# MLP down projections of an encoder trunk as 2x2 blocks with seven products (Strassen), MLP in four quarters of ff, weight sums on GpSimd

## The reference, cut to what matters

```python
D_MODEL, SEQ, DEPTH, D_FF = 1024, 512, 2, 4096      # float32 throughout

def squared_relu_mlp(h, w_in, w_out):
    u = jnp.square(jax.nn.relu(jnp.einsum('bsd,df->bsf', h, w_in)))
    return jnp.einsum('bsf,fd->bsd', u, w_out)

def reference(x, ...):
    for i in range(DEPTH):
        h = rms_norm(x, mix_norm[i])
        x = x + (neighbourhood_attention if i % 2 == 0 else sliding_window_gqa)(h, ...)
        h = rms_norm(x, mlp_norm[i])
        x = x + squared_relu_mlp(h, mlp_w_in[i], mlp_w_out[i])
    return rms_norm(x, final_norm)
```

## Time and profile before

| what | value |
|---|---|
| time, median of 3 runs | 1123.13 us (1123.12 to 1123.52) |
| profiled execution, first to last instruction (span) | 1121.9 us |
| time of runs less span | 1.2 us |
| PE busy | 1111.0 us, 5412 matmuls |
| DVE, ACT, POOL busy | 624.5, 521.0, 144.0 us |
| granted TensorE clock, mean | 0.998 |

### The profile page before, as it was taken

How to read it: one execution, slowest core, us unless ns; L and a number is a source line. 1 busy time by engine, 2 the same in 40 slices (tenths; PEclk the granted TensorE clock), 3 DMA queues, 4 the chain that set the end, 5 groups by cost and what they waited for, 6 DMA issues and landing times.

```text
span 1121.9 us, 16256 instructions
## 1 busy us (share of the span) xinstructions
PE 1111.0 (99%) x5412; PEld 925.6 (83%) x5412; DVE 624.5 (56%) x997; ACT 521.0 (46%) x921; POOL 144.0 (13%) x252
## 2 busy tenths in 40 slices
PE   8999999999999999999999999999999999999997
PEld 6888888888888888888888888888888888888886
DVE  7778887764442234443436799875443223444333
ACT  6777767654431124442325788744442112443222
POOL 6544332240000000000000244200000000000000
PEclk9999999999999999999999999999999999999999
DMA  6332322342223322222232223232222232222222
GB/s 225 101 93 75 112 75 74 94 121 94 93 94 100 104 96 94 93 93 96 91 112 91 65 86 85 72 122 94 93 93 94 96 102 102 93 93 94 93 93 94
DMA packets 37122, 109.09 MB, mean 97 GB/s; under 512 B 6544, under 2 KB 10928, under 8 KB 37088
## 3 DMA queue, kind: packets, MB, share of 16 engines
q1 hardware_dynamic: 32176, 100.74, 26.7%
q0 software_dynamic: 4768, 7.90, 3.1%
q10 hardware_dynamic: 144, 0.02, 0.0%
HBM read 105.93 MB, written 2.70 MB: 97 GB/s over the span
## 4 chain that ended last, share of the span: by engine, by line
PE 97%; DVE 1%; issue 0%; DMA 0%; ACT 0%; SPq 0%; DVEq 0%; ACTq 0%
PE acc L490 27%; PE acc L492 27%; PE acc L491 27%; PE acc L524 3%; PE om_ps L808 2%; PE pt_ps L795 1%; PE om_ps L643 1%; PE s_ps L606 1%; PE pt_ps L627 1%; PE s_ps L784 1%; PE om_ps L596 1%; PE s_ps L785 1%; PE s_ps L490 1%; PE s_ps L492 1%; PE s_ps L491 1%
## 5 line engine op out<-in xcount | busy, mean ns | idle before, releaser
L909 ACT CAST w_hi<-w_raw 128x1024 fp32r<-128x1024 f32 x179 | 188.0, 1050 | 388.1 <-PE acc L492 382.4
L1238 DVE TENSOR_TENSOR w_lo<-w_raw,w_hi 128x1024 fp32r<-128x1024 f32 x177 | 216.3, 1222 | 143.6 <-ACT w_hi L909 143.6
L490 PE MATMUL acc<-h_hi,w_hi 128*128 128x512 f32 x736 | 291.3, 396 | 0.9 <-DVE w_lo L1238 0.9
L492 PE MATMUL acc<-h_hi,w_lo 128*128 128x512 f32 x736 | 286.9, 390 | 0.0
L491 PE MATMUL acc<-h_lo,w_hi 128*128 128x512 f32 x736 | 286.5, 389 | 0.0
L490 PE MATMUL acc<-u_hi,w_hi 128*128 128x512 f32 (+1 forms) x624 | 240.4, 385 | 0.0
L492 PE MATMUL acc<-u_hi,w_lo 128*128 128x512 f32 (+1 forms) x624 | 239.5, 384 | 0.0
L491 PE MATMUL acc<-u_lo,w_hi 128*128 128x512 f32 (+1 forms) x624 | 239.4, 384 | 0.0
L490 PEld LDWEIGHTS acc<-h_hi,w_hi 128*128 128x128 f32 x736 | 138.3, 188 | 31.6 <-DVE w_lo L1238 1.6
L492 PEld LDWEIGHTS acc<-h_hi,w_lo 128*128 128x128 f32 x736 | 138.1, 188 | 29.2
L491 PEld LDWEIGHTS acc<-h_lo,w_hi 128*128 128x128 f32 x736 | 138.5, 188 | 28.3 <-issue 0.7
(11 more groups left out here) (171 smaller groups left out, 1119.8 us busy)
## 6 DMA issues: line engine op xcount, KB each, us to landing
w_raw<-in_wstream SPq DMA_DIRECT2D x180, 512.0 KB, 3.3
bias_pairs<-rpb_reversed POOLq DMA_DIRECT2D x64, 62.0 KB, 2.4
bias_pairs<-t_shifted POOLq DMA_DIRECT2D x64, 48.0 KB, 2.1
x_res<-in_xT SPq DMA_DIRECT2D x8, 256.0 KB, 5.9
vT<-inverse_sums SPq DMA_DIRECT2D x16, 128.0 KB, 3.0
out_y<-x_res SPq DMA_DIRECT2D x10, 128.0 KB, 1.8
out_y<-x_res SPq DMA_DIRECT2D x3, 256.0 KB, 2.4
inverse_sums<-sw_turned SPq DMA_DIRECT2D x32, 1.0 KB
```

The source lines that it names most:

```text
L490: nc.tensor.matmul(dst, a[0], b[0], start=start, stop=False)
L492: return nc.tensor.matmul(dst, a[1], b[0], start=False, stop=stop)
L909: nc.scalar.copy(w_hi[:, c.odd, :], w_raw[:, c.odd, :]).then_inc(w_hi_made, 1)
L1238: nc.vector.tensor_tensor(w_lo[:, c.odd, :], w_raw[:, c.odd, :], f32(w_hi[:, c.odd, :]), ALU.subtract).then_inc(w_split, 1)
```

## The change

The two halves of ff become four quarters of 8 hidden tiles. In each quarter the down projection (8 output tiles, 8 hidden tiles, 512 tokens) is a 2x2 block product: a group is two output tiles (i = 0, 1), the hidden tiles are four pairs, and the tokens are two halves of 256 (j = 0, 1). Instead of eight block products a group makes seven runs, with sums of weight blocks and of hidden blocks as operands. A run is 4 pairs x 3 matmuls, 256 tokens wide. Four groups make a quarter, 28 runs, in the order written by `run_order`. Some runs resume the bank of an earlier one, so that their sum is what DVE reads.

- POOL (`first_sums`) makes four sums of 128x512 for each group from the two raw chunks. ACT (`group_high`) casts 3.5 chunks' worth for a group instead of 2, in four pieces; DVE (`group_low`) subtracts as much.
- For each pair of hidden tiles DVE makes the sums (`hidden_sums`, three instructions) and low parts in three pieces (`hidden_low`), ACT the high parts in three pieces (`hidden_high`).
- DVE takes seven results of 128x256 for each group (`take_run`). Run 1's results gather in a buffer of their own; POOL adds them to x in the last quarter (`add_first_run`).
- Hidden stages have 9, 8, 8 and 7 tiles: each but the last ends with the first tile of the next quarter. Its result is taken in the last cycle of the runs.
- Raw weights of groups 0 and 2 go to a new buffer `d_raw`, those of groups 1 and 3 to `w_raw`. The high and low weights have two halves, which chunks and groups use in turn.
- After the first MLP two chunks of the sliding-window projections run interleaved (`two_after_norm`), and POOL adds the squares for that norm (`add_square`). The loads of the sliding-window biases for the first two pairs move on POOL's queue from before the first MLP to behind it.
- The end: run 3 of the last group has a bank of its own and comes last; the final norm's statistics of tiles 6 and 7 come from it and the runs before.
- All MLP loops are unrolled. Several buffers of the attention stages share room with the new ones.

```diff
+IN_STAGES = [range(0, 9), range(9, 17), range(17, 25), range(25, 32)]
+WEIGHTS_PIECE = {1: 1, 2: 1, 5: 2, 6: 2, 7: 3, 3: 3, 4: 4}
+HIDDEN_PIECE = {1: 1, 2: 2, 3: 2, 4: 3, 5: 3, 6: 3, 7: 3}
+def run_order(m, q):
+    order = [(0, 1), (0, 6), (0, 5), (0, 2), (0, 7)]
+    for g in range(1, GROUPS):
+        order += [(g, 1), (g, 6), (g - 1, 4), (g - 1, 3), (g, 5), (g, 7), (g, 2)]
+    order += [(3, 3), (3, 4)]
+    if (m, q) == (1, 3):
+        order[-9:] = [(3, 1), (3, 6), (2, 4), (3, 2), (3, 7), (2, 3), (3, 4), (3, 5), (3, 3)]
+    return order
...
+            def load_group(m, q, g):
+                gi = 16 * m + 4 * q + g
+                if gi >= 2:
+                    sp.wait_ge(d_split, 4 * gi - 4)
...
+                if g == 1:
+                    sp.wait_ge(w_split, (CH_MLP0, CH_MLP1)[m] + IN_STAGES[q][-1] + 1)
+                for i in range(2):
+                    sp.dma_start(raw_rows(q, g)[:, i, :], wstream[out_place(m, q, 2 * g + i)]).then_inc(d_landed[g % 2][i], 16)
...
+            def first_sums(m, q, g):
+                gi, raw = 16 * m + 4 * q + g, raw_rows(q, g)
+                if gi >= 1:
+                    pool.wait_ge(d_split, 4 * gi - 1)
+                pool.wait_ge(d_landed[g % 2][1], 16 * (gi // 2 + 1))
+                nc.gpsimd.tensor_tensor(w_sums[:, 0:QUAD], raw[:, 1, 0:QUAD], raw[:, 1, QUAD:2 * QUAD], ALU.add).then_inc(sums_made, 1)
...
+                nc.gpsimd.tensor_tensor(w_sums[:, QUAD:2 * QUAD], w_sums[:, 0:QUAD], raw[:, 0, 0:QUAD], ALU.subtract).then_inc(sums_ended, 1)
+                nc.gpsimd.tensor_tensor(w_sums[:, 2 * QUAD:3 * QUAD], raw[:, 0, 0:QUAD], raw[:, 1, 0:QUAD],
+                                        ALU.subtract).then_inc(sums_made, 1)
+                pool.wait_ge(sums_ended, 2 * gi + 1)
+                nc.gpsimd.tensor_tensor(w_sums[:, 3 * QUAD:4 * QUAD], raw[:, 0, QUAD:2 * QUAD], w_sums[:, QUAD:2 * QUAD],
+                                        ALU.subtract).then_inc(sums_ended, 1)
...
+            def mlp(m):
...
+                for q in range(QUARTERS):
+                    ends = q == QUARTERS - 1
+                    first_sums(m, q, 0)
+                    first_sums(m, q, 1)
+                    for g in range(GROUPS):
+                        if ends:
+                            add_first_run(m, g)
+                            if g and m == 0:
+                                add_square(2, 2 * g - 2)
+                                add_square(2, 2 * g - 1)
+                        if g < GROUPS - 2:
+                            first_sums(m, q, g + 2)
...
+            def run(m, q, g, r):
...
+                pe.wait_ge(d_split, 4 * gi + WEIGHTS_PIECE[r])
+                before = {2: 1, 7: 6, 4: 7, 3: 5}
...
+                elif r in before:
+                    pe.wait_ge(run_taken, RUN[quarter, g, before[r]])
+                elif gi >= 2:
+                    pe.wait_ge(run_taken, RUN[(gi - 2) // 4, (gi - 2) % 4, {1: 2, 6: 4, 5: 3}[r]])
+                for k in range(PAIRS_K):
+                    if g == 0:
+                        pe.wait_ge(u_split, 3 * (4 * quarter + k) + HIDDEN_PIECE[r])
...
+                    ins = product(bank, (parts[:, 0, :], parts[:, 1, :]), (uh[:, k, other, :], ul[:, k, other, :]),
+                                  k == 0 and (parted or r not in before), k == PAIRS_K - 1, r in before and not parted)
...
+            def hidden_sums(m, n):
...
+                nc.vector.tensor_tensor(t_sums[:, 0:4:2, :], hidden[:, at:at + 2, FEW:SEQ], first.rearrange("p (j t) -> p j t", j=2),
+                                        ALU.subtract).then_inc(hidden_summed, 1)
...
+                nc.vector.tensor_tensor(t_sums[:, 1, :], second[:, FEW:SEQ], t_sums[:, 0, :], ALU.subtract).then_inc(hidden_summed, 1)
...
+                nc.vector.tensor_tensor(t_sums[:, 3, :], second[:, 0:FEW], t_sums[:, 1, :], ALU.subtract).then_inc(hidden_summed, 1)
...
+            def hidden_low(m, n):
...
+                nc.vector.tensor_tensor(ul[:, k, 0, :], first[:, 0:FEW], f32(uh[:, k, 0, :]), ALU.subtract).then_inc(u_split, 1)
...
+                nc.vector.tensor_tensor(ul[:, k, 1:3, :], second.rearrange("p (j t) -> p j t", j=2), f32(uh[:, k, 1:3, :]),
+                                        ALU.subtract).then_inc(u_split, 1)
...
+                nc.vector.tensor_tensor(ul[:, k, 3:7, :], t_sums, f32(uh[:, k, 3:7, :]), ALU.subtract).then_inc(u_split, 1)
...
+                    for i, (g, r) in enumerate(run_order(m, q)):
...
+                        slot = i - at
+                        if cycle < GROUPS - 1:
+                            if slot in (1, 2) or slot == 3 and cycle == 0:
+                                group_low(m, q, cycle + 1, slot)
+                            elif cycle and slot in (4, 5):
+                                group_low(m, q, cycle + 1, slot - 1)
...
+                        take_run(m, q, g, r)
+            def two_after_norm(c, g, n):
...
+                for k in range(6):
+                    part(c + 1, g + 1, h_tile, [k])
+                    if k == 2:
+                        statistics(n)
+                for k in range(6, KT):
+                    pe.wait_ge(h_low, KT * n + k + 1)
+                    part(c, g, h_tile, [k])
+                    part(c + 1, g + 1, h_tile, [k])
```

More of the change, by code:

```diff
@@ L697, in output_projection @@
                     part(At(ch + EARLY + n), At(gr + EARLY + n), u_tile, ALL)
[L699 to L725, removed]
@@ L727, in last_statistics, with first_statistic_of_last @@
-            def last_statistics(n):
[L729 to L732, removed]
+            def first_statistic_of_last():
+                pe.wait_ge(h_split, KT * NORMS - 2)
+                pe.wait_ge(pool_filled, 4)
+                for n in range(2):
+                    for b in range(2):
+                        nc.tensor.matmul(last_stats[n], sqsum[:, (2 * n + b) * P:(2 * n + b + 1) * P],
+                                         pick[:, 1 - b:3 - b], start=b == 0, stop=False)
@@ L733, in last_statistics @@
+            def last_statistics(n):
+                pe.wait_ge(x_prepared, KT * NORMS + 2 * n)
+                for k in range(2):
+                    for b in range(2):
+                        ins = nc.tensor.matmul(last_stats[n], last_square[:, k, (2 * n + b) * P:(2 * n + b + 1) * P],
+                                               pick[:, 1 - b:3 - b], start=False, stop=k == 1 and b == 1)
                 ins.then_inc(stat_done, 1)
@@ new lines, in mlp @@
+            def mlp(m, norm):
+                c0 = (CH_MLP0, CH_MLP1)[m]
+                for q, stage in enumerate(IN_STAGES):
+                    for n in stage:
+                        c = At(c0 + n)
+                        if n == 0:
+                            part_after_norm(c, c, norm)
+                        else:
+                            part(c, c, h_tile, ALL, weights=(chunk_parts(0, q % 2)[:, c.odd, :], chunk_parts(1, q % 2)[:, c.odd, :]))
+                    for g, r in run_order(m, q):
+                        if (m, q, g, r) == (1, 3, 3, 3):
+                            first_statistic_of_last()
+                            last_statistics(0)
+                        run(m, q, g, r)
+                if m == 1:
+                    spread_rstd(0)
+                    last_statistics(1)
+                    spread_rstd(1)
@@ new lines, in square, with hidden_high @@
+            def square(m, n):
+                c = (CH_MLP0, CH_MLP1)[m] + n
+                at = hidden[:, n % 4, :]
+                act.wait_ge(acc_taken, c + 1)
+                nc.scalar.activation(at, at, ACT.Square).then_inc(squared, 1)
+            def hidden_high(m, n):
+                pair, k = 16 * m + n // 2, n // 2 % PAIRS_K
+                first, second = hidden[:, n % 4 - 1, :], hidden[:, n % 4, :]
+                act.wait_ge(squared, 32 * m + n + 1)
+                if n >= 8:
+                    act.wait_ge(run_done, RUNS * (4 * m + n // 8))
+                nc.scalar.copy(uh[:, k, 0, :], first[:, 0:FEW]).then_inc(u_hi_made, 1)
+                nc.scalar.copy(uh[:, k, 1:3, :], second.rearrange("p (j t) -> p j t", j=2)).then_inc(u_hi_made, 1)
+                act.wait_ge(hidden_summed, 3 * pair + 3)
+                nc.scalar.copy(uh[:, k, 3:7, :], t_sums).then_inc(u_hi_made, 1)
@@ L1447, in last_norm @@
-                add(0)
-                reciprocal(0)
-                for k in range(4):
-                    result(0, k)
-                add(1)
-                for k in range(4, KT):
-                    result(0, k)
+                    dve.wait_ge(x_gained, KT - 2 + 2 * n + (2 if end == KT else 0))
+                    nc.vector.tensor_tensor(x[:, k:end, t], x[:, k:end, t], spread[:, 0:end - k, :], ALU.mult).then_inc(y_made, end - k)
+                reciprocal(0)
+                for k, end in FIRST_STORES[0:2]:
+                    result(0, k, end)
```

564 lines of the change are left out of this document (371 added, 193 removed).

## The result

| | before | after |
|---|---|---|
| time, median | 1123.25 us (1123.12 to 1123.52) | 1127.1 us (1126.51 to 1129.33, 5 runs) |
| ratio after / before | | 1.0036, interval 1.0023 to 1.0048 |
| profiled execution, span | 1121.9 us | 1126.0 us (its time 1127.71) |
| granted TensorE clock, mean | 0.998 | 0.990 |

The change makes the kernel 0.36% slower. The forecast was 1117 us, with "faster" as the likeliest outcome. The time lies inside the wide range (1105 to 1132), but above the forecast's own range (1110 to 1125), and the change goes the other way than was forecast.

A forecast was written before the change was run, and what follows sets the result against it. PE was taken to bound the MLPs, by number and width of matmuls. -27.3 + 7.8 + 7.0 + 0 + 3.0 + 1.9 + 1.6 = -6.0 us gave 1117.1 us; own range 1110 to 1125, wide range 1105 to 1132.

The forecast's parts named there:

- saving: Down projections: 1488 wide and 96 narrow matmuls, 348.8 us, become 2688 narrow ones, 321.5 us: -27.3 us.
- starts, quarters 0 to 2: PE waits for hidden sums and low parts at six run starts, 1.3 us each: 7.8 us (0 to 16.2).
- starts, quarter 3: PE waits 2.9 plus 0.6 us for the last hidden tile's chain at two run starts: 7.0 us (6 to 9).
- within the runs: PE waits behind POOL and DVE: 0 (0 to 3.0) in quarters 0 to 2, 3.0 us (0 to 7) in quarter 3.
- between the layers: PE waits for cast and low part after the interleaved chunks free a weight buffer late: 1.9 us (1 to 2.5).
- end: All results come behind the last run, so DVE ends later after the last matmul: +1.6 us (0.5 to 3).
- sum: All terms added over the whole kernel: -6.0 us, giving 1117.1 us from 1123.1.
- Rival C: At 224 run starts a whole matmul's time (0.12 us) is lost: 27 us more, 1144 us; chance 0.05.
- alone-case: Run starts with DVE's and ACT's chain undisturbed by POOL's sums: no wait in quarters 0 to 2, 3.5 us in quarter 3.
- rival B: POOL and DVE strictly take turns; 2.7 us per quarter start, 3.0 and 7.0 within runs: +9.4, 1132.5 us; chance 0.27.
- the exclusion: POOL's sums and DVE's low parts, both inputs in SBUF, exclude each other: 9.3 of a group's 10.05 us booked.

The follow-up runs named there:

- experiment 1: Changed kernel with POOL's weight sums cut to 2 columns instead of 512 in all but each layer's first group: 1109.59 us.
- experiment 2: Changed kernel with POOL's sums of group 1 held back until the low parts of the quarter's last hidden pair are made: 1140.55 us.
- Experiment 3: Changed kernel with 36 extra narrow matmuls into an unused bank during PE's wait at the start of each layer's quarter 3: 1128.5 us.
- experiment 8: Changed kernel with pairs 0 to 2 of runs 1, 6 and 5 ahead of run 1's last pair in the last quarters: 1127.83 us.
- Experiment 5: Changed kernel with POOL's full-size sums kept but unread except in each layer's last group; ACT and DVE cut raw weights instead: 1125.87 us.
- experiment 7: Changed kernel with group 1's weight sums made by DVE, POOL keeping those of groups 0, 2 and 3: 1118.79 us.
- experiment 6: Changed kernel with the weight sums of groups 1 to 3 made by DVE, POOL keeping group 0's: 1119.96 us.
- experiment 4: Changed kernel with the first interleaved chunk's last two blocks ahead of the second's, after the first MLP: 1126.5 us in one execution.
- experiment 9: Changed kernel with DVE making sums of group 1 in quarters 0 to 2, groups 1 to 3 in the last; some instructions moved: 1118.89 us.
- experiment 11: As experiment 9, but DVE makes the sums of groups 1 to 3 in all quarters: 1119.19 us.

## Why the prediction was wrong, step by step

The stretches of narrow matmuls are compared with the shortest that a quarter takes, 40.31 us for 336 of them, as in the six quarters of experiment 1 that have no wait.

| step | forecast | measured |
|---|---|---|
| saving | -27.3 | 8 x 40.31 = 322.5 against 348.8: -26.3 |
| starts, quarters 0 to 2 | 7.8 | 0.3 + 1.8 + 1.7 + 1.7 + 0 + 1.8 = 7.3 |
| starts, quarter 3 | 7.0 | 2 x 4.8 of wait, about 2 x 2.2 behind it at half clock: 14 |
| within the runs | 0 and 3.0 | 1.3 and 2.1 |
| between the layers | 1.9 | 2.11 between two matmul starts instead of 0.23: 1.9 |
| end | 1.6 | last matmul to end 10.3 instead of 8.4: 1.9; the last run at half clock: 1.0 |
| sum | -6.0 | +3.2; the spans differ by 4.1 |

- **The saving** was right: 0.1200 us a narrow matmul, waits or not. Rival C is refuted.
- **The step that failed is the start of quarter 3**, forecast at 7.0 us and measured at 14, which is 7.0 of the 9.2 us that the sum is off. The prediction let the chain of the last hidden tile run alone, as if POOL's sums of group 1 were over. They are not: they don't wait for their weights, which have long landed, but for the low part of group 0's third piece, which frees `w_sums`; it ends at 538.8, and POOL starts at 538.90, 0.95 us before the stage's end. That gate was in the code: first_sums waits for `d_split` of the group before. Even without it the prediction's own landing times (-3.4 to -1.9) put the end of four sums at 1.7 to 3.2, inside its chain of 0.9 to 3.9. The alone-case stands in experiments 1 and 2: a first wait of 2.4 us (forecast 2.9), 3.2 in all (forecast 3.5). With POOL in it the first wait is 4.65.
- **Behind it the clock fell** to 0.50 for some 23 matmuls, twice, which the sum had no term for. Experiment 3 shows that at this place it is a symptom more than a price: with the clock held the time was no better, as DVE's queue was next. It may not be free everywhere: of the changed kernel's five executions the two with a mean clock of 0.995 took 1126.5 and 1126.6 us, the three with 0.990 took 1127.1 to 1129.3.
- **The sum itself** added waits as if each were paid for. In the last quarter they are not: experiments 3 and 8 shorten its start and gain nothing. Start and runs of the two last quarters together cost 16.1 us where 7.0 + 3.0 were forecast.
- **Starts of quarters 0 to 2**: the middle of the bounds, 1.3 us each, came out as 1.2 on average. That is partly luck, as no start is near the middle: four cost 1.7 to 1.8, two 0 to 0.3. Which it is follows from when group 1's weights land, as the prediction had it. POOL's first sum began 3.1 to 3.2 us before the stage's end in the four, 2.04 and 1.89 before it in the two:

```profile
370.92 1.29 POOL L566 TENSOR_TENSOR room<-w_raw 128x512 f32<-128x512 f32 x1 [32.61 <-DMA w_raw<-in_wstream]
287.86 1.30 POOL L566 TENSOR_TENSOR room<-w_raw 128x512 f32<-128x512 f32 x1 [30.27 <-DMA w_raw<-in_wstream]
```

The stages end at 374.08 and 289.90. The mechanism, turns with POOL, was right, and so were the forecast lengths (DVE over 1.3 us, POOL 1.3 to 2.5). The Trainium skill (SBUF — State Buffer, section "SBUF: two separate sides") says that the lock on the pair of ports that the two engines share holds for a whole instruction; the trace agrees, with 0.41 us against 1.37 for the same width. The turns (rival B's rule) do occur wherever POOL has four sums in a row. B overrated what they cost PE: 1.7 to 1.8 at four starts and nearly nothing at two, where it had 2.7 at all six; 1.3 of 3.0 within quarters 0 to 2, 2.1 of 7.0 within the last ones.
- **What POOL's weight sums cost in all** is 17.5 us by experiment 1, against some 11 that the sum had for the exclusion: two thirds of what the seven products save. Experiment 5 shows 16.3 of it as exclusion. POOL's additions and squares of the last quarter are not in this: DVE's low parts of h still take 1.50 us in experiment 1.
- **The end**: the chain of results is 0.3 us longer than said. The last run at half clock (0.59 in the window from 1113 to 1116) is 1 us more. In experiment 1, with the same statistics ahead of it, that run had the full clock, so the order of the end alone doesn't bring it about; why it came stays open.

Still open besides: 0.9 us of the span's difference, and whether the last quarter can be freed of its waits. That may need work taken off DVE there altogether, such as the next norm's low parts. Nor did any run put the take of run 7 ahead of the next group's fourth low part in DVE's program, though that take is what PE waits for within the runs of the changed kernel.

The best version is that of experiment 7: 1118.8 us, 0.4% under the kernel before. Some 22 of the 26 us saved are given back even so, most of them in the last quarters: in experiment 6, of nearly the same time, their narrow stretches take 49.5 and 46.9 us (the second without its last run) where 40.3 and 38.9 would do.

## What to carry to other kernels

Work given to GpSimd is not free for VectorE: count the time of GpSimd's additions and of VectorE's instructions with two inputs in SBUF as one queue, and where they meet a latency chain, the chain pays a whole GpSimd instruction per link. If VectorE does the same sum in half the time, moving it there shortens that queue even when VectorE is the busier engine. A filled gap on a fast engine is worth nothing until the next queue behind it has slack: in the last quarter keeping the clock up and reordering the products each gained nothing. And where one engine both makes operands and empties the banks, a late operand holds up the banks that stand behind it in the written order.

## What the runs showed of the hardware

- GpSimd and VectorE take strict turns when both ask. In the changed kernel's trace from 255 us on, no VectorE instruction with two SBUF inputs has more than one POOL addition end inside it, and no POOL addition has more than one such VectorE instruction end inside it. POOL's last sum averaged 1.99 us over 32 (1.27 in a gap), DVE's 1024 wide low part 1.46 over 64 (1.22) and its 512 wide one 1.20 over 16 (0.68). VectorE's takes, with one input in PSUM, stayed at 0.41 to 0.42 throughout.
- After each of the six waits of 4.6 us at the start of a last quarter (the changed kernel, experiments 4 and 5) TensorE worked at 1.2 GHz for three to five us. After the twelve of 2.4 us at the same place (experiments 1, 2, 6, 7, 9 and 11) it was at 2.4 GHz in seven cases and fell to 1.2 in five (layer 0 of 6, 9 and 11, layer 1 of 7 and 9). So the shorter wait doesn't keep the clock for sure. The same wait in layer 1, first in experiment 6, then in experiment 7 (clock 1.00 and 0.50):

```profile
1060.00:1065.00 5.00, 3.76 (x27) 3.35 (x27) 4.73 (x9) 2.76 (x3) 0.00 (x0) 1.00 0.04 16
```
```profile
1063.90:1067.00 3.10, 3.07 (x14) 3.07 (x15) 2.83 (x5) 1.67 (x2) 0.00 (x0) 0.50 0.08 32
```

- TensorE holds 0.1200 us a matmul of 256 columns, each with new weights, in runs of 12 into alternating banks; the change of bank costs nothing that can be seen (40.31 us for 336 in experiment 1).
